# Hybrid decoder trunk in fp32: oT_hi and oT_lo allocated directly behind the weight rings

## What is computed

```python
def swiglu(x, wg, wu, wd):
    return (jax.nn.silu(x @ wg) * (x @ wu)) @ wd

for i in range(DEPTH):
    g = norm_g[i]
    x = x + 0.5 * rmsnorm(swiglu(rmsnorm(x, g[0]), ffn1_wg[i], ffn1_wu[i], ffn1_wd[i]), g[1])
    xn = rmsnorm(x, g[2])
    mixer, j = i % N_MIXERS, i // N_MIXERS      # 0 conv, 1 attention, 2 mLSTM
    ...
    x = x + rmsnorm(y, g[3])
    x = x + 0.5 * rmsnorm(swiglu(rmsnorm(x, g[4]), ffn2_wg[i], ffn2_wu[i], ffn2_wd[i]), g[5])
```

## Time and profile before

| | us |
|---|---|
| median of 3 runs | 2140.26 (2139.55 to 2142.18) |
| span of the profiled execution | 2140.2 |
| PE busy | 2108.0 (98%) |
| PE weight loads busy | 1931.7 (90%) |
| DVE busy | 1185.7 (55%) |
| ACT busy | 965.4 (45%) |
| DMA, mean | 180 GB/s |

### The profile page before, as it was taken

The page is one execution under the profiler, slowest core; times in us unless marked ns, Lnnn a source line. Parts: engine busy times, 40 slices in busy tenths (PEclk is TensorE's granted clock), DMA queues, the critical chain, the costliest instruction groups (busy, mean ns, idle before and its releaser), DMA issues.

```text
span 2140.2 us, 35887 instructions
## 1 busy us (share of the span) xinstructions
PE 2108.0 (98%) x14636; PEld 1931.7 (90%) x14636; DVE 1185.7 (55%) x1346; ACT 965.4 (45%) x1177; POOL 52.5 (2%) x100
## 2 busy tenths in 40 slices
PE   8999999999998999999999999999999999999998
PEld 6998989988998998997999899898999899898997
DVE  5555765456456554555645654555645654576543
ACT  5444544344435544454444543554444543544442
POOL 0000000000000000000000000000000000000000
PEclk9999999999999999999999999999999999999999
DMA  8554655546554342342644545453644555455551
GB/s 317 185 191 167 221 185 203 206 160 216 194 185 172 124 153 100 119 158 94 232 186 179 206 187 203 153 193 134 231 185 178 205 188 203 154 212 187 205 187 60
DMA packets 55981, 386.27 MB, mean 180 GB/s; under 512 B 6592, under 2 KB 7104, under 8 KB 10816
## 3 DMA queue, kind: packets, MB, share of 16 engines
q1 hardware_dynamic: 52416, 372.53, 47.2%
q10 hardware_dynamic: 3456, 12.13, 1.6%
HBM read 383.58 MB, written 1.05 MB: 180 GB/s over the span
## 4 chain that ended last, share of the span: by engine, by line
PE 98%; ACT 1%; DVE 0%; issue 0%; DMA 0%; POOL 0%; POOLq 0%; ACTq 0%; DVEq 0%
PE ps L407 29%; PE ps L409 29%; PE ps L408 29%; PE ps L420 2%; PE ps L423 2%; PE ps L426 2%; PE ps L687 1%; PE ps L712 1%; PE ps L700 1%; PE ps L442 1%; PE ps L689 0%; PE ps L674 0%; PE ps L714 0%; ACT xT_high L905 0%; PE ps L497 0%
## 5 line engine op out<-in xcount | busy, mean ns | idle before, releaser
L1219 DVE TENSOR_TENSOR w_low<-raw,w_high 128x2048 fp32r<-128x2048 f32 x352 | 804.2, 2289 | 321.3 <-ACT w_high L881 321.1
L407 PE MATMUL ps<-xT_high,w_high 128*128 128x256 f32 x2656 | 736.0, 277 | 0.0
L409 PE MATMUL ps<-xT_high,w_low 128*128 128x256 f32 x2656 | 734.9, 277 | 0.0
L408 PE MATMUL ps<-xT_low,w_high 128*128 128x256 f32 x2656 | 734.5, 277 | 0.0
L881 ACT ACTIVATE w_high<-raw 128x2048 fp32r<-128x2048 f32 x352 | 670.7, 1911 | 37.7 <-DMA raw<-stream 21.1
L408 PEld LDWEIGHTS ps<-xT_low,w_high 128*128 128x128 f32 x2656 | 499.4, 188 | 2.7
L407 PEld LDWEIGHTS ps<-xT_high,w_high 128*128 128x128 f32 x2656 | 499.0, 188 | 3.1
L409 PEld LDWEIGHTS ps<-xT_high,w_low 128*128 128x128 f32 x2656 | 498.6, 188 | 0.0
L916 ACT ACTIVATE region<-ps 128x256 f32<-128x256 f32 x176 | 67.6, 384 | 668.6 <-PE ps L409 651.3
L407 PE MATMUL ps<-w_high,oT_hi 128*128 128x512 f32 x832 | 330.4, 397 | 0.0
L409 PE MATMUL ps<-w_high,oT_lo 128*128 128x512 f32 x832 | 329.6, 396 | 0.0
(11 more groups left out here) (147 smaller groups left out, 1258.3 us busy)
## 6 DMA issues: line engine op xcount, KB each, us to landing
raw<-stream SPq DMA_DIRECT2D x352, 1024.0 KB, 4.8
gain<-gains ACTq DMA_DIRECT2D x23, 512.0 KB, 4.7
x<-x_in SPq DMA_DIRECT2D x2, 512.0 KB, 6.0
out<-x SPq DMA_DIRECT2D x2, 512.0 KB, 2.6
gain<-gains SPq DMA_DIRECT2D x1, 512.0 KB, 5.3
att_mask<-att_mask_in SPq DMA_DIRECT2D x1, 384.0 KB, 5.1
rope<-rope_in SPq DMA_DIRECT2D x1, 128.0 KB, 4.5
ml_mask<-ml_mask_in SPq DMA_DIRECT2D x1, 128.0 KB, 4.9
```

The costliest lines, as they stand in the source:

```text
L407: nc.tensor.matmul(acc, lh, rh, start=start, stop=False)
L408: nc.tensor.matmul(acc, lh, rl, start=False, stop=False)
L409: return nc.tensor.matmul(acc, ll, rh, start=False, stop=stop)
L1219: nc.vector.tensor_tensor(w_low[:, p % RING, :], raw[:, p % RAW, :], w_high[:, p % RING, :], ALU.subtract).then_inc(piece_split, 1)
```

## The change

`oT_hi` and `oT_lo` are allocated directly behind `w_low`, instead of last. Nothing else in the program is changed, and each engine has the same instructions in the same order.

```diff
         w_high = sb("w_high", [P, RING, PIECE], F32R)
         w_low = sb("w_low", [P, RING, PIECE], F32R)
 
+        oT_hi = sb("oT_hi", [P, KD, SEQ], F32R)
+        oT_lo = sb("oT_lo", [P, KD, SEQ], F32R)
         x = sb("x", [P, TILES, D])
...
         gate_bias = sb("gate_bias", [P, 2 * NH])
 
-
-        oT_hi = sb("oT_hi", [P, KD, SEQ], F32R)
-        oT_lo = sb("oT_lo", [P, KD, SEQ], F32R)
```

## The result

The changed kernel takes 2150.4 us (median of 5 runs, 2148.55 to 2151.61) against 2140.33 us; the ratio is 1.0043, 95% interval 1.0031 to 1.0054. The forecast was 2127 us, and 0.58 for faster. Its own span in the profile is 2148.0 us, 7.8 more than before.

A forecast was written before the change was run, and what follows sets the result against it. PE's own matmul pace was taken as the bound (98% of the span). 2496 oT matmuls at 5.3 ns less make 13.2 us, all else priced 0: 2140.3 - 13 = 2127 us, range 2104 to 2155.

The forecast's parts named there:

- The bound: Whole kernel: PE works 98% of the span, so only its start-to-start matmul pace can move the time.
- Where the price sits: 512-column matmuls at full clock: 234.2 ns with oT stationary, 228.9 with xT, so the stationary tile's address can have a price.
- The rule of independent read ports: TensorE operand reads: moving and stationary use two independent ports, so the change does nothing and the time stays 2140.
- The rule of 16-byte lines: SBUF start addresses: lines are 16 bytes and both oT starts fall on one, so the time stays 2140.
- The price of one: The 2496 oT matmuls: losing the odd 32 bytes gives xT's pace, 5.3 ns less each, 13.2 us less.
- The tiles behind it. Price 0.: x, xn, gain, xT, ident, region and the rest move up 16,384 bytes, keeping their remainders over 1024: price 0.
- the bounds paragraph: oT matmuls: 35 us less at the 256-column form's 6.7 ns loss, 22 us more at one 8.9 ns step up.
- Coincidence costs: oT matmuls: stationary and moving reads starting on the same remainder compete, pace over 234.2 ns; 2155 us, chance 0.25.
- Coincidence helps: oT matmuls: reads in step leave only 6.7 ns loss, 220.0 ns each; 2105 us, chance 0.22.
- Nothing: oT matmuls: pace decided by how a run is entered or something else, not by the change; 2140 us, chance 0.17.
- xT's forms keep 228.9 and 113.3 and the whole gain sits in the oT runs: Sign of being right: projection's oT matmuls at 228.9 ns, 21.75 us instead of 22.25, with xT's paces unchanged.
- Whole addresses count: xT's forms change too: Sign in the xT matmuls: if their paces change, whole addresses matter and the sum is wrong in kind, not size.

The follow-up runs named there:

- e2: Kernel before, oT still last but behind 32 unused bytes, on a multiple of 64 and not the rings' remainder: 2136.02 us, ratio 0.9972.
- e1: Kernel before, oT still last but behind 160 unused bytes, on the rings' remainder over 512, no other tile moved: 2150.48 us, ratio 1.0042.
- g1: The kernel of f3 with xT moved to the end, at 704 over a multiple of 1024 (192 over 256): 2153.61 us, ratio 1.0058.
- e8: Kernel before, oT last behind 192 unused bytes, 32 bytes behind the rings' class: 2140.05 us, ratio 0.9993.
- e5: Kernel before, last product of each oT run that a block follows made in two halves of 256 columns: 2143.17 us, ratio 1.0012.
- e7: Kernel before, oT last behind 352 unused bytes, at xT's remainder (320 over 512): 2130.00 us in 2 runs, ratio 0.9946.
- f3: Changed kernel, only the very last matmul of each oT run that a block follows split in two of 256 columns: 2123.97 us, ratio 0.9914.
- g3: The same kernel as f3, measured once more with five runs: 2123.68 us, ratio 0.9917.
- run 4: Changed kernel plus one 128x128 transpose of the identity behind each oT run that a block follows (64 of them): 2130.04 us, ratio 0.9944.

## Why the prediction was wrong, point by point

**The bound.** Right: PE's own pace decides, and every difference between these kernels was found in start-to-start distances. PE's waits stayed within some 0.4 us of the earlier trace rows, but for one on w_low, 0.5 to 1.8 us from trace to trace.

**Where the price sits.** Right in kind: the pace of a 512-column matmul depends on where its stationary tile starts, and moving oT alone changed oT's pace. The rule of independent read ports (Trainium skill, "TensorE: Matmul & The Clock Gate", "Step-by-step: what each phase is for") would have left 2140, but the traces have the same form in the same order at 234.2 ns before and 226.7 after. What they contradict is that addresses cost nothing; whether the two reads meet somewhere was not measured. The rule of 16-byte lines (Trainium skill, "SBUF — State Buffer", "Door 1: The DMA port swizzle") would have left it too: all starts tried fall on such a line, and five paces of the 512-column form came of them.

**The price of one.** Mis-sized, and by a wrong reason. The term was 2496 x 5.3 ns = 13.2 us and measured 17.7: 7.6 ns for each matmul in a steady run, 7.1 with the first ones of each run. The reason was the odd 32 bytes, and run e2 removes them alone for 1.9 ns. What counts is d over 256, and xT's 228.9 was merely another d. That a shift by 512 does nothing was right; by the same rows I could have asked for a shorter period and did not.

**"The tiles behind it. Price 0."** Right for the tiles, as run e1 shows, where they do not move and everything else is the same. But this is where the sum ends, and it has no term for the same instructions at the same addresses. **This is the step that failed:** I priced the edited matmuls and held all others fixed, although the bounds paragraph had said that the 256-column form has two paces that the remainder does not decide. I used that only as a bound for oT, and never asked who might change places between them. 6528 block matmuls stood directly behind the ones that changed. They cost 26.9 us, which is more than the gain of 17.7.

**The rivals.** "Coincidence costs" named the sign and, with 2155, nearly the time, but not the mechanism: it wanted oT over 234.2, and oT is at 226.7. "Coincidence helps" was half right for oT (226.7, not 220.0). In 220.0 I carried over the 6.7 ns loss of the blocks; equal starts cost 13.3 ns each. "Nothing" had the sentence that turned out to matter, that a pace is decided by how a run is entered.

**The signs.** "xT's forms keep 228.9 and 113.3 and the whole gain sits in the oT runs" was the test, and it failed, in the FFN blocks only. That, with the convolution's 113.3 in the same trace, is what pointed to inheritance. "Whole addresses count: xT's forms change too" was a bad sign: xT's forms did change, and run e1 shows the same with xT where it was.

**The range.** 2104 to 2155 held the time, but the direction was wrong. That the range held is luck: its upper end stood for slower oT matmuls, and these became faster.

**A reading in passing.** The half clock of the earlier trace rows is read from the pace alone; the trace's clock records begin at 17.5 us, and before that the views print 1.00. Two later stretches bear it out: where the same trace records a granted clock of 0.50 (from 666.0 us for 6.8 us, from 826.5 us for 3.4), token-first matmuls of 256 columns are mostly 213 to 214 ns apart, and 256 columns at 1.2 GHz are 213.3.

## What to carry to other kernels

Where PE is the bound and float32r matmuls run back to back, the start of the stationary and of the moving tile over 256 bytes is a parameter to tune per form: here equal starts were best for 512 moving columns and worst for 256. A change to one form's pace has to be checked in the form that follows it without a pause, since that may inherit a slower pace, and a single matmul of another width at the seam can undo it, as it did here at d = 64 and did not at d = 192. So sum start-to-start distances by form over the whole trace, before and after, and not only over the lines that were edited.

## What was not expected of the hardware

- A run of equal matmuls can hold either of two steady paces with the same tiles, 113.3 and 117.8 ns for 256 columns and 228.9 and 233.3 for 512, over as many as 384 matmuls. What held it is seen only in a side effect: in the slow blocks of the changed kernel every third weight load, that of w_low, is recorded at 192 ns instead of 188 (mean 191 in the group above), and in g1's slow blocks not even that. Which part of TensorE or of the memory keeps the pace was not found.
- Behind an oT run of 226.7 ns a block stayed at 117.8 in all 64 runs of the FFNs, of 48, 96 and 192 matmuls; behind 228.9, 232.4, 233.3 and 234.3 all of the longer ones, of 96 and 192, went to 113.3. After a split or a transpose in the changed kernel all 64 did. The runs of 48 are less firm: behind 233.3 (e8) and behind the split of e5 all eight were at 117.8. Why just the fastest oT run leaves the slow pace behind is open.
- Some runs of matmuls elsewhere, such as the 384 of a convolution, were at either pace from trace to trace (113.3 in both convolutions of e1, 117.8 in both of e7), and the program does not decide it. Runs f3 and g3 are the same kernel, and they have it the other way round. Their first convolutions, 360 steps each, f3 and then g3:

```profile
225.11 0.28 PE L406 MATMUL ps<-xT_high,w_high 128*128 128x256 f32 x1
...
265.91 0.28 PE L406 MATMUL ps<-xT_high,w_high 128*128 128x256 f32 x1
```

```profile
226.88 0.28 PE L406 MATMUL ps<-xT_high,w_high 128*128 128x256 f32 x1
...
269.28 0.28 PE L406 MATMUL ps<-xT_high,w_high 128*128 128x256 f32 x1
```

These are 113.3 and 117.8 ns; in the second convolution f3 has 117.8 and g3 113.3. The two traces are from two chips; what decides is not shown. Each such run stands behind eight transposes, and before these stands a piece of 48 matmuls of the same form. In the twelve traces with xT in its old class, all 24 runs of 384 have the pace of their 48, which is 113.3 in 14 and 117.8 in 10. So a slow pace can outlive eight transposes, and the single transpose of run 4 is not a cure everywhere. The premise of run 4, that blocks behind transposes run at 113.3 in both traces, had missed the second convolution of the kernel before, at 117.8.

- At 384 x 4.4 ns = 1.7 us for each convolution, this is a spread of some us that belongs to no edit and that a single profile does not average out. The clock adds to it: f3's trace has 6.8 us at the half clock before its last microseconds, and g3's, of the same kernel, 13.7.
